# Value products with the values stationary in two column groups, outputs turned back inside later units, and products of constants between the steps of the first attention

## What is computed

```python
s = einsum('bqhcd,bkhcd->bhcqk', q, k) * (A_QK ** -0.5)
p = softmax(s, axis=-1)
a = p[:, :, 0] - lam * p[:, :, 1]
o = einsum('bhqk,bkhd->bqhd', a, v)          # then an rmsnorm of each head's 64 columns
```

```python
p = softmax(concatenate([s_win + bias, s_ctx]), axis=-1)
o = p_win @ v_rows + p_ctx @ v_ctx
```

## Time and profile before

| | |
|---|---|
| median of 3 runs | 1337.29 us (1320.17 to 1338.97) |
| the profiled execution | 1334.26 us, span of its profile 1332.2 us |
| mean granted TensorE clock | 0.954 of full |
| PE busy | 1220.0 us, 92% of the span |
| DVE busy | 862.2 us, 65% |
| ACT busy | 588.6 us, 44% |

### The profile page before, as it was taken

How to read it: one execution, slowest core, us unless ns; L and a number is a source line. 1 busy time by engine, 2 the same in 40 slices (tenths; PEclk the granted TensorE clock), 3 DMA queues, 4 the chain that set the end, 5 groups by cost and what they waited for, 6 DMA issues and landing times.

```text
span 1332.2 us, 16908 instructions
## 1 busy us (share of the span) xinstructions
PE 1220.0 (92%) x6412; PEld 899.1 (67%) x6412; DVE 862.2 (65%) x1282; ACT 588.6 (44%) x781; POOL 129.2 (10%) x126
## 2 busy tenths in 40 slices
PE   6999999968799995899999999889999898989996
PEld 1444474857688764788888888648877777765774
DVE  3479788768775447588898888664337555734543
ACT  1540010335555524487777787343333443334422
POOL 1101101000122000011221111300000000000000
PEclk9999999988799997899999999999999899899998
DMA  8735656770130053699999999652343445544301
GB/s 360 279 134 221 237 234 224 182 158 1 56 147 1 0 201 136 237 359 392 408 411 398 408 409 401 247 197 78 110 172 108 145 169 155 167 144 157 126 0 63
DMA packets 52822, 267.52 MB, mean 201 GB/s; under 512 B 15031, under 2 KB 22071, under 8 KB 38040
## 3 DMA queue, kind: packets, MB, share of 16 engines
q1 hardware_dynamic: 38264, 205.85, 42.1%
q0 software_dynamic: 9744, 47.19, 9.8%
q10 hardware_dynamic: 4752, 13.63, 2.7%
HBM read 226.80 MB, written 36.70 MB: 198 GB/s over the span
## 4 chain that ended last, share of the span: by engine, by line
PE 74%; DVE 13%; ACT 5%; DMA 3%; issue 3%; SPq 2%; POOL 1%; DVEq 0%; ACTq 0%; POOLq 0%
PE PS L2772 21%; PE PS L3196 7%; PE PS L3197 7%; PE PS L3198 7%; PE PS L3110 3%; PE PS L3422 3%; PE PS L3423 3%; PE PS L3424 3%; PE PS L3328 2%; PE PS L3327 2%; PE PS L3329 2%; PE PS L3064 2%; PE PS L3408 1%; SPq L804 1%; PE PS L2789 1%
## 5 line engine op out<-in xcount | busy, mean ns | idle before, releaser
L1394 ACT ACTIVATE arena_r<-ring 128x2048 fp32r<-128x2048 f32 x100 | 185.9, 1910 | 11.7 <-ACT arena L1431 7.4
L2772 PE MATMUL PS<-arena 128*128 128x64 f32 (+6 forms) x674 | 150.1, 390 | 30.0 <-DMA arena<-in_small_f_w 7.6
L2223 DVE TENSOR_TENSOR arena_r<-ring,arena_r 128x2048 fp32r<-128x2048 f32 x66 | 148.2, 2286 | 20.3 <-ACT arena_r L1394 19.7
L2772 PEld LDWEIGHTS PS<-arena 128*128 128x128 f32 (+2 forms) x674 | 100.2, 205 | 73.9 <-issue 40.5
L2772 PE MATMUL PS<-hT,ring 128*128 128x512 f32 (+1 forms) x304 | 118.9, 549 | 0.0
L3196 PE MATMUL PS<-arena_r,hT_r 128*128 128x512 f32 x272 | 112.4, 413 | 4.9 <-DVE hT_r L2405 4.9
L3422 PE MATMUL PS<-arena_r 128*128 128x512 f32 x256 | 104.7, 409 | 13.0 <-DVE ring_r L2631 8.5
L3197 PE MATMUL PS<-arena_r,hT_r 128*128 128x512 f32 x272 | 108.9, 400 | 0.0
L3424 PE MATMUL PS<-arena_r,ring_r 128*128 128x512 f32 x256 | 101.8, 398 | 0.0
L1203 ACT ACTIVATE arena<-PS 128x1024 f32<-128x1024 f32 (+2 forms) x31 | 28.5, 927 | 159.7 <-PE PS L2772 144.7
L2772 PEld LDWEIGHTS PS<-hT,ring 128*128 128x128 f32 x304 | 57.1, 190 | 59.0 <-issue 57.4
(11 more groups left out here) (481 smaller groups left out, 2416.0 us busy)
## 6 DMA issues: line engine op xcount, KB each, us to landing
ring<-in_moe SPq DMA_DIRECT2D x51, 2048.0 KB, 10.5
ring<-in_slabs SPq DMA_DIRECT2D x27, 2048.0 KB, 8.9
ring<-in_slabs SPq DMA_DIRECT2D x9, 1024.0 KB, 5.5
y_rows<-arena ACTq DMA_DIRECT2D x16, 512.0 KB, 10.0
ssm_scratch<-arena POOLq DMA_DIRECT2D x4, 1152.0 KB, 5.1
arena<-ssm_scratch POOLq DMA_DIRECT2D x4, 1152.0 KB, 8.3
ssm_scratch<-arena POOLq DMA_DIRECT2D x4, 1024.0 KB, 10.9
y_rows<-in_tab_no_token SPq DMA_DIRECT2D x1, 4096.0 KB, 25.1
```

The costliest lines, as they stand in the source:

```text
L1394: nc.scalar.activation(rounded(moe_w_hi[n][:, cols]), ring[:, n, cols], ACT.Copy).then_inc(s_moe_hi[n], 1)
L2223: nc.vector.tensor_tensor(rounded(moe_w_lo[n][:, cols]), ring[:, n, cols], as_float(moe_w_hi[n][:, cols]), ALU.subtract).then_inc(s_moe_lo ...
L2772: ins = nc.tensor.matmul(out, lhsT, rhs, start=(n == 0), stop=(n == len(pairs) - 1))
```

## The change

- In `a` and `b` the unit `("o", i)` becomes `("v", i)`: the values (64 columns) are stationary and the transposed probabilities (128 columns) move. The six pieces alternate between column groups 0 to 63 and 64 to 127, so that the slot holds two half sums on top of each other, with 128 queries along the columns. ACT copies it to `o_T` (128x128, three buffers).
- A later unit turns the output back: one product with `o_T` stationary and `halves_sum` (two 64x64 identities on top of each other) moving gives 128 queries x 64 columns and adds the halves. In `a` that of i-2 stands in `("t", i)`, in `b` that of i-3 in `("s", i)`, behind the unit's own products, in columns of the slot that were free. One more unit `("o", 15)` at the end of each attention takes the last two or three.
- In `a` ACT (instead of DVE) scales the outputs, behind its copy of the transposes. In `b` DVE still does (`output_b`), now between adding the bias and the row maximum of `("s", i)`, and waits for its own result before the maximum (`s_scaled`, which takes the place of `s_prob` too).
- `keep_clock(out, n)` issues n fp32 products of constants (ones, 128x128, with 256 columns of `vec`): 8 ahead of the wait in the first inverse, and in `a` ahead of the wait of each `("t", i)`: 9 for i = 0, 1 for i = 1, 4 and 8, else 2. Their results are overwritten or not read.

The diff, with context left out:

```diff
@@ -87,6 +87,7 @@
 CONV_AT = {1: 0, 4: 1, 8: 2, 15: 3}
+FILL, FILL_STEP = {0: 9, 1: 1, 4: 1, 8: 1}, 2
@@ -111,10 +112,12 @@
         if behind:
-            yield ("o", i - 1)
+            yield ("v" if a != "g" else "o", i - 1)
         if a == "a" and i == n:
             yield ("conv", len(SECOND_CONV) - 1)
+    if a != "g":
+        yield ("o", n - 1)
@@ -131,7 +134,14 @@
         turn = turn[0:2]
-    return (a, *turn), ("dve" if kind == "o" else "act")
+    return (a, *turn), ("dve" if kind == "o" and a != "a" else "act")
+def outputs_in(a, kind, i, n):
+    if a == "a":
+        return [n - 2, n - 1] if kind == "o" else [i - 2] if i >= 2 else []
+    return [n - 3, n - 2, n - 1] if kind == "o" else [i - 3] if i >= 3 else []
@@ -372,6 +382,7 @@
         k_hi_b, k_lo_b = region(R_FWD, [2, TC]), region(R_FWD + 2 * TC, [2, TC])
+        o_T, halves_sum = rstd[:, 0:3 * P].rearrange("p (a b) -> p a b", a=3), rstd[:, 3 * P:3 * P + VD]
         o_a = region(R_QKV + 1024, [QT, 256])
@@ -622,7 +633,7 @@
         s_max = sem("s_max")
-        s_prob = sem("s_prob")
+        s_scaled = sem("s_scaled")
         s_o = sem("s_o")
@@ -1308,6 +1319,17 @@
             n = QT * HEADS
+            def outputs(a, key):
+                for m, o in enumerate(outputs_in(a, key[1], key[2], n)):
+                    qt, h = o // HEADS, o % HEADS
+                    act.wait_ge(s_scaled, o + 1)
+                    first = (0 if key[1] == "o" else TC) + VD * m
+                    ins = nc.scalar.activation(o_a[:, qt, VD * h:VD * h + VD], both(key)[:, first:first + VD], ACT.Copy,
+                                               scale=stat[:, 2 * o % 8, 3:4])
+                return ins
             for a in ("a", "b"):
@@ -1329,17 +1351,20 @@
-                            filled(act, ("a", "o", n - 1))
+                            filled(act, ("a", "v", n - 1))
                         nc.scalar.activation(prob_b[turn[1]], both(key)[:, 0:TC], ACT.Exp, bias=stat[:, j % 8, 0:1], scale=1.0,
-                            filled(act, (a, "o", i - 1))
+                            filled(act, (a, "v", i - 1))
                         elif a == "b":
-                            filled(act, ("a", "o", n - 1))
-                        nc.scalar.activation(probT_a if a == "a" else probT_b, both(key)[:, 0:TC], ACT.Copy).then_inc(s_act_read, 1)
+                            filled(act, ("a", "v", n - 1))
+                        ins = nc.scalar.activation(probT_a if a == "a" else probT_b, both(key)[:, 0:TC], ACT.Copy)
+                        if a == "a" and i >= 2:
+                            ins = outputs(a, key)
+                        ins.then_inc(s_act_read, 1)
                         if a == "b":
@@ -1347,9 +1372,14 @@
                             forward_odd(*key[1:])
-                    elif turn[0] == "o":
+                    elif turn[0] == "v":
+                        filled(act, key)
+                        nc.scalar.activation(o_T[:, i % 3], bank(key, 0)[:, 0:P], ACT.Copy).then_inc(s_act_read, 1)
                         if a == "a":
                             high_b(i)
+                    elif turn[0] == "o" and a == "a":
+                        filled(act, key)
+                        outputs(a, key).then_inc(s_act_read, 1)
                     elif turn[0] == "pm":
@@ -2096,6 +2126,9 @@
                     then(nc.vector.tensor_tensor(bank(key, 0), bank(key, 0), bias_b[:, h, first:first + T], ALU.add))
+                    if i >= 3:
+                        output_b(key, i - 3)
+                        dve.wait_ge(s_scaled, n + i - 2)
                 nc.vector.tensor_reduce(stat[:, j % 8, 0:1], both(key)[:, 0:TC], AX_X, ALU.max,
@@ -2107,27 +2140,21 @@
                 nc.vector.scalar_tensor_tensor(out=prob_a[:, i % 2, 0], in0=prob_a[:, i % 2, 1], scalar=stat[:, j + 1, 3:4],
-                                               in1=prob_a[:, i % 2, 0], op0=ALU.mult, op1=ALU.add).then_inc(s_prob, 1)
-            def output(a, i):
-                qt, h = i // HEADS, i % HEADS
-                key = (a, "o", i)
-                if a == "a":
-                    filled(dve, key)
-                    nc.vector.tensor_scalar(o_a[:, qt, VD * h:VD * h + VD], bank(key, 0)[:, 0:VD],
-                                            stat[:, 2 * i % 8, 3:4], None, ALU.mult).then_inc(s_dve_read, 1)
-                else:
-                    dst = post[:, qt % 2, VD * h:VD * h + VD]
-                    if h == 0 and qt >= 2:
-                        filled(dve, (a, "ot", qt - 2))
-                    j = (2 * n + i) % 8
-                    read(dve, (a, "s", i, 0))
-                    then(nc.vector.reciprocal(stat[:, j, 3:4], stat[:, j, 1:2]))
-                    filled(dve, key)
-                    nc.vector.tensor_scalar(dst, bank(key, 0)[:, 0:VD], stat[:, j, 3:4], None,
-                                            ALU.mult).then_inc(s_dve_read, 1)
+                                               in1=prob_a[:, i % 2, 0], op0=ALU.mult, op1=ALU.add).then_inc(s_scaled, 1)
+            def output_b(key, o):
+                qt, h = o // HEADS, o % HEADS
+                if h == 0 and qt >= 2:
+                    filled(dve, ("b", "ot", qt - 2))
+                j = (2 * n + o) % 8
+                m = outputs_in("b", key[1], key[2], n).index(o)
+                first = (0 if key[1] == "o" else TC) + VD * m
+                read(dve, ("b", "s", o, 0))
+                then(nc.vector.reciprocal(stat[:, j, 3:4], stat[:, j, 1:2]))
+                return nc.vector.tensor_scalar(post[:, qt % 2, VD * h:VD * h + VD], both(key)[:, first:first + VD],
+                                               stat[:, j, 3:4], None, ALU.mult).then_inc(s_scaled, 1)
@@ -2148,6 +2175,7 @@
+            then(nc.vector.tensor_tensor(halves_sum, ident[:, 0:VD], ident[:, VD:2 * VD], ALU.add))
             for c in range(2):
@@ -2165,8 +2193,6 @@
                         gated(*at)
-                if i >= 1:
-                    output("a", i - 1)
                 if i - 1 in CONV_AT:
@@ -2191,7 +2217,6 @@
                     row_max("b", i + 1, 0, 2 * n + i + 1)
-                output("b", i - 1)
                 if i == 2:
@@ -2199,6 +2224,11 @@
                     mix_low({11: 1, 12: 2, 14: 3, 15: 4, 16: 5}[i])
+            filled(dve, ("b", "o", n - 1))
+            for o in range(n - 3, n):
+                output_b(("b", "o", n - 1), o)
+            dve.wait_ge(s_scaled, 2 * n)
+            dve.sem_inc(s_dve_read, 1)
             for part in range(6, 9):
@@ -2774,6 +2804,11 @@
+            def keep_clock(out, n):
+                for _ in range(n):
+                    nc.tensor.matmul(out[:, 0:NVEC], ones[:], vec[:], start=True, stop=True)
             def ada(j):
@@ -2990,7 +3025,8 @@
                 start_unit(key)
+                if (o, c) == (0, 0):
+                    keep_clock(bank(key, 0), 8)
                 pe.wait_ge(s_spec, FT * (o + 1))
@@ -3034,15 +3070,26 @@
                         pairs = [(q_h, k_h), (q_l, k_h), (q_h, k_l)]
-                    products(out, [(rounded(x), rounded(y)) for x, y in pairs], last=(half == 1))
+                    ins = products(out, [(rounded(x), rounded(y)) for x, y in pairs])
+                if a == "b" and i >= 3:
+                    ins = outputs(a, key)
+                ins.then_inc(s_filled, 1)
                 start_unit(key)
-                read(pe, ("b", "o", HEADS * qt + HEADS - 1))
+                pe.wait_ge(s_scaled, n + HEADS * qt + HEADS)
                 for c in range(2):
                 ins.then_inc(s_filled, 1)
+            def outputs(a, key):
+                for m, o in enumerate(outputs_in(a, key[1], key[2], n)):
+                    read(pe, (a, "v", o))
+                    first = (0 if key[1] == "o" else TC) + VD * m
+                    ins = nc.tensor.matmul(both(key)[:, first:first + VD], o_T[:, o % 3], halves_sum, start=True, stop=True)
+                return ins
@@ -3056,20 +3103,29 @@
                         if a == "a":
-                            pe.wait_ge(s_prob, i + 1)
+                            keep_clock(bank(key, 1)[:, TC - T:], FILL.get(i, FILL_STEP))
+                            pe.wait_ge(s_scaled, i + 1)
                         else:
                             ins = nc.tensor.transpose(both(key)[:, P * t:P * t + P], p[:, P * t:P * t + P], ident[:])
+                        if a == "a" and i >= 2:
+                            ins = outputs(a, key)
                         ins.then_inc(s_filled, 1)
-                    elif turn[0] == "o":
+                    elif turn[0] == "v":
                         start_unit(key)
                         v, pT = (v_a, probT_a) if a == "a" else (v_b, probT_b)
-                        products(bank(key, 0)[:, 0:VD],
-                                 [(pT[:, P * t:P * t + P], v[:, t, VD * h:VD * h + VD]) for t in range(KT)], last=True)
+                        for t in range(KT):
+                            c = t % 2
```

(6 more changed lines are left out.)

## The result

The changed kernel takes 1350.75 us (median of 4 runs, 1348.26 to 1353.69); the kernel before, 1336.05 (4 runs, 1320.17 to 1338.97). The ratio is 1.0127, 95% interval 1.009 to 1.0164. So the change costs 14.7 us where +4.7 was forecast. The profiled execution took 1350.52, its span is 1348.6 (before: 1332.2), +16.4.

A forecast was written before the change was run, and what follows sets the result against it. The prediction saw PE on 74% of the chain but priced the change by loops through PE, DVE and ACT: -1.6 - 0.8 + 1.0 + 2.8 + 0.8 + 2.2 + 0.6 = +5.0, so 1342 us, range 1322 to 1351.

The forecast's parts named there:

- Value product: Both attentions: the twelve value instructions take 0.80 us in place of 1.36, saving 0.56.
- Output: Both attentions: turning one output back costs PE 0.23 us, leaving a net PE saving of 0.33 a step.
- First inverse, -1.6: Ahead of the first attention: eight products of constants fill 3.5 us of PE's wait and hold the clock, -1.6 us.
- Nine products "fit into the 4.87": First attention, step 0: nine products of constants (3.9 us) fit PE's 4.87 wait before the first transposes; step gets back 1.0.
- Plain step 4.30: First attention at full clock: a plain step takes 4.30 us against 3.83, +1.9 over four intervals.
- DVE's four convolution intervals, -1.1: First attention: four intervals with convolution work are DVE's, which loses the scaling (0.27 each), -1.1 us.
- Hand-over, +2.8: Between the attentions: `mean_a` begins at 383.2 and the second attention's first value product comes at 387.0, +2.8 us.
- The clock after it, 0 to +2, taken +0.8: Behind the hand-over: PE idles about 2.5 us without products of constants, so the clock may fall, +0.8 us.
- Second attention, +2.2: Second attention: the two-step loop goes from 7.11 to 7.43 us, +0.16 a step, +2.2 over 14 steps.
- the clock rival, at 0.08: Second attention: the clock falls; a third of the steps cost +9, total 1351, at most 1369; chance 0.08.
- Tail, +0.6: Second attention's end: a copy, an output and three DVE pairs stand behind the last value product, +0.6 us.
- PE's saving counts in full: Both attentions: ACT's and DVE's new work finds cover and the clock holds, about -10 us, 1328; chance 0.25.

The follow-up runs named there:

- experiment 10: Changed kernel, second-attention outputs one unit later, first attention's last outputs ahead of the last inverse, constants only ahead of the first inverse: 1340.4 us, ratio 1.0062.
- experiment 1: Changed kernel with the second attention in its old form, so the change in the first attention only: 1362.14 us, ratio 1.0185.
- experiment 2: Changed kernel with second-attention outputs turned back one unit later, with a fourth `o_T` buffer: 1352.69 us, ratio 1.0115.
- experiment 3: Changed kernel with the first attention's last two outputs ahead of the last inverse instead of behind it: 1343.62 us, ratio 1.007.
- experiment 6: Changed kernel with the second attention in its old form and the first attention's last outputs ahead of the last inverse: 1336.61 us, ratio 1.0027.
- experiment 8: Changed kernel, second-attention outputs one unit later, first's last ones ahead of the last inverse, one product of constants per second-attention step: 1345.23 us, ratio 1.0076.
- experiment 4: Changed kernel without any products of constants: 1346.62 us, ratio 1.0095.
- experiment 5: Kernel before with one wait added, `mean_a` starting only when the last inverse's unit is filled: 1363.47 us, ratio 1.0224.
- experiment 9: Kernel before with `mean_a` made to wait for the last inverse, plus four products of constants in PE's idle time there: 1334.46 us, ratio 0.9998.

## Why the prediction was wrong, and where it was right

It had the verdict right (a loss within 2%) and the size wrong by 10 us: +4.7 forecast, +14.7 measured. The step that failed most is the second attention: forecast at +2.2, it took +9.4, of which 6.4 is its loop at full clock (plain steps of 3.92 for 3.7, and three of 5.01 with a unit more, which it did not price), and 3.2 the clock, for which the sum had nothing. Next comes what the clock does behind the hand-over. By its own steps:

- **Value product**: 0.80 forecast; 0.81 in experiment 10. Right. **Output**: 0.23 forecast. It is 0.36 ahead of a value product in two column groups (384.99 to 385.35), and in the first attention, where full-width scores follow, 0.14 (last section). So PE saves less than 0.33 a step: from one value product to the next the step was 3.38 before (394.88 to 398.26), without a wait; against 3.22 that is 0.16. The Trainium skill (TensorEngine Tiling (Array Packing), Tiling Modes, Key Properties) says that a change of the tiling mode drains TensorE; the prediction put this at 0.04 a step by the row at hand. The traces agree in direction, a dense step falls short by 0.17, but no run sets the mode change apart from the rest. It did not decide the result.
- **First inverse, -1.6**: not obtained in the changed kernel's trace (8.86), obtained in the nine others with the eight products (7.17). The mechanism was right; that one execution missed it.
- **Nine products "fit into the 4.87"**: failed. The row of before shows PE idle for 4.87, but their slot is free only after 2.65 of it. They cost 0.5 in step 0 at full clock, and 2.2 to 3.5 when it falls under them, as it did in five of seven traces (experiments 1, 2, 3, 6 and 8). With that, first combine to last was +1.6 where -0.8 + 1.0 was forecast.
- **Plain step 4.30**: 4.33 measured. Right, and experiment 4 (3.95) shows the 0.4 to be the constants. The wait behind the forward transforms was forecast at 2.6 and was 1.71. That the clock falls there more often than not was right: in the changed kernel's trace it fell behind the second of the two only (340.6), in experiments 1, 2, 3, 6 and 8 behind both.
- **DVE's four convolution intervals, -1.1**: -1.6 (29.18 against 30.79 in all).
- **Hand-over, +2.8**: +3.4 from the last combine to the value product, `mean_a` at 382.95 for 383.2, idle time 2.60 for 2.5. Right within 0.6. **The clock after it, 0 to +2, taken +0.8**: failed. Such idle time cost 29 us with the old second attention (experiment 5), where the clock stayed down for 58 us. With the new one it stayed down for 6.9 and 10.2 us (experiments 2 and 4), and in the changed kernel's trace it fell only 12 us later. Experiment 3's 7 us, known to some 6, is what the order of that unit costs on average, hand-over and clock together; 2.8 + 0.8 was forecast.
- **Second attention, +2.2**: +9.4. Two causes. The larger, +6.4: the prediction followed only the two-step loop, extended by the new operations (7.43; 7.58 in experiment 10, so rightly). It priced the output at 0.23, and did not ask what it waits for: that ties s(i) to ACT's instruction behind the exponential of s(i-1), one step long, 3.92 against the forecast's 3.7. Nor did it look at the three steps with a unit more, where the scores wait for their slot (5.01; 5.01 to 5.05 in experiment 10 too, so one unit later does not help them). The smaller, +3.2: **the clock rival, at 0.08**, came true in part, four low steps that cost 4.9 (less 1.6 that the clock cost before). For its rejection it cited a stretch of the first attention with 3.83 of 5 busy at full clock; one stretch that held was no evidence that a loop holds. That its time, 1351, came out is luck: it had +9 for the clock and hardly more than the sum's +2.2 for the loop.
- **Tail, +0.6**: +1.4, with ACT's copy, the output unit and the three pairs on DVE in a row.
- **"PE's saving counts in full" (0.25)**: wrong even for experiment 10, where the hand-over's idle time and the one-step loop are gone.

What stays open: whether the first attention's new value product gains anything in all (0.9941 to 1.0002), why the clock falls at 398.7 in one trace and at 415.9 in another with the same second attention (the changed kernel and experiment 3), and why it comes back after 3.4 us in the old second attention of the kernel before (423.6 to 427.0), after 6.9 and 10.2 in the new one (experiments 2 and 4), and only after 54.6 and 58.0 in experiments 1 and 5.

## What to carry to other kernels

An operation added to a unit ties that unit to everything that the operation waits for: look for loops that close in one step, not only for the loop that binds now. Saving PE's work in a loop that waits elsewhere makes PE idle, and idle time just ahead of a dense loop can cost over ten times its length (2.00 us, 29 us), since the clock falls and the loop, slower but without a wait, can take 55 us to bring it back; a few useless products in exactly that gap, in a slot that is free, cost nothing and returned it all. The same products in steps that have no gap cost 4 to 7 us here. And before a loss is put down to the clock, the same steps have to be found at full clock: most of this one was the loop.

## What the runs showed of the hardware

- The same instructions ran at two speeds: the second attention's old step took 3.5 us at granted clock 1.00 with PE busy 9.53 of 10 (experiment 9), and 6.25 at 0.50 with PE busy 10.00 of 10 (experiments 1 and 5), for some 55 us. Being busy without a pause did not raise the clock there; under a PE just as busy it came back after 10.2 us in the new form (8.00 of 8 us, experiment 4) and after 3.4 in the old form of the kernel before (5.87 of 5.87 us). The Trainium skill (TensorE: Matmul & The Clock Gate, Part 4) says that transposes do not count as busy for it in the same way; both speeds of the old form have the same share of them, so no run here tells whether that is why.
- Idle times of 2.00 (experiment 5), 2.60 (experiments 1 and 2) and 2.59 (4) were followed within 1 us by the lower clock, or it fell in them, while the 2.60 in the changed kernel's trace was followed by full clock for 12 us. Waits of 1.05 to 1.07 in the new loop were followed by it four times (389.70 and 410.00 in experiment 10, 403.05 and 423.35 in experiment 2) and twice not (435.69 and 449.04).
- A product of two instructions takes 0.36 from its start to the next unit's when a unit in two column groups follows (384.99 to 385.35, experiment 10), and 0.14 when full-width scores follow:

```profile
305.42 0.33 PE L3091 MATMUL PS<-rstd 128*128 128x64 f32 x2
...
305.56 1.31 PE L2802 MATMUL PS<-ring_r 128*128 128x512 f32 x4
```

That is the changed kernel's timeline in the first attention; the difference is 0.22. What stands ahead of the output differs too (scores with 64 rows in experiment 10, full-width transposes here), so that not all of it need be the price of going into two column groups; no run sets the two apart.
